# ScalarE takes a convolution's unshifted tap and two levels of copies; heads are squared and gated out of PSUM, and output norms start from partial sums

## The chip, the cores and the metric

One core of one Trainium2 chip. The metric is the device time of the whole program in microseconds (us), the median of several runs. Everything is float32; TensorE's large products are split in software into a "high" and a "low" half (`h_high`, `h_low`, `w_high`, `w_low`), three matmuls for each block.

## The reference, cut to what matters

Four layers run on a sequence of 256 tokens of width 1024: an HGRN-2 mixer, an RG-LRU mixer (each followed by a product-key expert layer), then an "even" mixer (gated delta rule beside dilated attention) and an "odd" mixer (differential attention beside gated linear attention, GLA), each followed by a convolutional feed-forward layer. The pieces that the change touches:

```python
# HGRN-2 (8 heads, both directions) and GLA (4 heads): decayed attention by chunks
attn = sum_k(q[t, k] * k[s, k] * decay[t, s, k]);  o = attn @ v + carried state
o = rms_norm(o, norm_g) * silu(g);  y = o @ w_out
# delta rule: q, k, v pass a causal convolution of width 4 before everything else
y = w[0] * xp[:, :seq];  for j in 1..3: y = y + w[j] * xp[:, j:j + seq]
o_a = rms_norm_2(o_a, norm_w) * silu(z_a);  mix = concatenate([o_a, o_b]) @ w_out
# after an output product: residual and norm
x = x + g1 * y;  h = rms_norm(x, g) * (1 + sc) + sh          # hg_out, lru_out
h = layer_norm(ALPHA * h + mix, g, b)                        # even_out, odd_out
```

## The kernel before

The activations lie transposed: 128 features on the partitions, 256 tokens (`T`) along the free axis, eight chunks (`DC`) for the width. Weights come from memory as tiles of 128x1024 through a ring of four (SP's queue). For a split product ScalarE writes `w_high` of tile k+2 (`split_high`, two halves, each as soon as half of tile k is used), VectorE subtracts to get `w_low` (`split_low`), and TensorE runs 24 matmuls (`passes`, L528 to L530) for the tile into one of four PSUM slots. There is no planner around the change: each engine runs one fixed list of instructions, and semaphores tie the lists together.

**Decayed attention** (`decay_attention`, used for HGRN-2 as `HG` and for GLA). The score matrix of a chunk of 128 tokens is built from a diagonal and seven levels of blocks, for HG once for each of two directions; a last step crosses the two chunks. For each step n TensorE computes scores (L670) into `PB` or `PA` by turns. VectorE multiplies keys and queries by the decay of the next level (`spread`, L1851 to L1860, which waits until the scores that used them are done) and moves the blocks of the level out of PSUM under a mask (`select`, L1873). ScalarE copies only the crossing scores (L1271). Then TensorE computes the output (L682, L686) into `PA`. In order after it: VectorE copies `PA` to SBUF (L2438, for GLA L2394), ScalarE squares the copy (L1191), TensorE sums the squares (L619), ScalarE takes the root (L1251), VectorE the reciprocal (L1803), TensorE spreads it over the partitions (L627), and VectorE multiplies each pair of heads by it (L1810), by gain and gate (L1817; L1815 for the differential heads), and splits it (`split_pair`, L1766) after ScalarE's L1165. TensorE waits for all pairs of L1810 before the output product starts. The delta rule ends in the same `head_norm`, with its squares taken from PSUM by ScalarE and its copy (L2324) beside the sums.

**The output products** (`hg_out`, `lru_out`, `even_out`, `odd_out`). VectorE adds each finished chunk to `X` (`add_product`, L1708 and L1709). For the first two ScalarE squares pairs of chunks (L1191) and TensorE adds up the eight chunks in eight matmuls against a matrix of 1/D (L602). For the last two the mean comes first (L611, eight matmuls over `X`), VectorE subtracts it (L1792), and then come squares and L602. A root (L1195), a reciprocal (L1758), a scaling and an affine step lead to the next product.

**The delta rule's convolution** (tiles 18 to 35 of the 42 of `even_in`). VectorE writes the unshifted tap of each tile from PSUM (L1686) and adds three shifted ones (L1684). In the tiles before, 0 to 17, ScalarE evacuates the product (L1414) and then splits the tile after next; some of both carry steps of the dilated attention. At tile 36 ScalarE waits for the last convolution and goes on with tables for Silu and the squares that lead to the delta rule.

## Time and profile before

| | us |
|---|---|
| median of 3 runs (lowest, highest) | 3133.36 (3130.40, 3135.28) |
| the profiled execution | 3136.99 |
| its span, first to last instruction | 3135.3 |
| TensorE busy | 2956.2 (94%) |
| VectorE busy | 2258.7 (72%) |
| ScalarE busy | 1614.1 (51%) |
| mean granted TensorE clock | 0.963 of full |

Busy times are sums over a span in which many stages follow each other; the granted clock is TensorE's, as a share of 2.4 GHz, and 0.50 is 1.2 GHz. The stages that the change touches lie at 200 to 345 us (HG and `hg_out`), 1300 to 1333 (`lru_out`), 2286 to 2390 (convolution), 2467 to 2515 (end of the delta rule, `even_out`) and 2826 to 2915 (GLA, `odd_out`).

### The profile page before, as it was taken

To read this page: it belongs to the slowest core of one execution; us is meant where nothing else is said; L and a number is where in the kernel's file an instruction comes from. 1 tells how busy PE (TensorE), PEld (TensorE's weight loads), DVE (VectorE), ACT (ScalarE), POOL (GpSimd) and SP (SyncE) were. 2 spreads that over 40 slices of the span, in tenths; PEclk is the share of its full clock that TensorE was granted. 3 is DMA by queue.
4 is the path that set the end of the run, shared out by engine and by line. 5 is a ranking of instruction groups with operands and counts; after the bars stand their busy time and mean duration, and the time that the engine had idled before them with its cause. 6 is when DMAs were issued, how large, how long until landed. Compare 5 with 4: busy or idle time off the path is not lost.

```text
span 3135.3 us, 57437 instructions
## 1 busy us (share of the span) xinstructions
PE 2956.2 (94%) x19454; PEld 2691.2 (86%) x19454; DVE 2258.7 (72%) x4758; ACT 1614.1 (51%) x3321; POOL 79.0 (3%) x120
## 2 busy tenths in 40 slices
PE   5997999999999999989999999999999889897898
PEld 4886899999887778889999988887898889796896
DVE  6337579888779984459888877777685578665686
ACT  1111557778644443455777854444543257462574
POOL 3000000000001100000000000000200000000000
PEclk8998999999999999999999999999899999997999
DMA  9520455444468863445444455554331145441453
GB/s 365 198 92 14 138 178 169 154 158 148 154 238 312 308 208 114 142 149 186 162 150 161 142 174 188 188 190 164 136 125 54 55 165 171 137 140 56 138 176 121
DMA packets 137685, 502.97 MB, mean 160 GB/s; under 512 B 15312, under 2 KB 15440, under 8 KB 137264
## 3 DMA queue, kind: packets, MB, share of 16 engines
q1 hardware_dynamic: 122544, 445.57, 41.8%
q0 software_dynamic: 14976, 55.19, 4.9%
q8 instruction: 106, 1.74, 0.2%
q14 instruction: 59, 0.48, 0.0%
HBM read 498.60 MB, written 2.10 MB: 160 GB/s over the span
## 4 chain that ended last, share of the span: by engine, by line
PE 81%; DVE 6%; ACT 3%; issue 1%; DVEq 0%; ACTq 0%
PE PB L528 13%; PE PB L530 13%; PE PB L529 13%; PE PA L570 9%; PE PA L572 9%; PE PA L571 9%; PE PA L722 4%; PE PB L518 3%; DVE w_low L2097 2%; PE PA L929 1%; PE PA L602 1%; PE PA L1092 1%; DVE BIG L2123 1%; ACT h_high L1234 1%; PE PB L929 1%
## 5 line engine op out<-in xcount | busy, mean ns | idle before, releaser
L1131 ACT ACTIVATE w_high<-ring 128x512 fp32r<-128x512 f32 x1532 | 953.4, 630 | 869.3 <-PE PA L572 466.9
L2097 DVE TENSOR_TENSOR w_low<-ring,w_high 128x512 fp32r<-128x512 f32 x1532 | 1047.8, 695 | 433.4 <-ACT w_high L1131 420.3
L528 PE MATMUL PB<-h_high,w_low 128*128 128x256 f32 x3728 | 1081.5, 290 | 48.6 <-DVE h_low L1766 35.8
L530 PE MATMUL PB<-h_high,w_high 128*128 128x256 f32 x3728 | 1059.2, 284 | 0.0
L529 PE MATMUL PB<-h_low,w_high 128*128 128x256 f32 x3728 | 1059.0, 284 | 0.0
L528 PEld LDWEIGHTS PB<-h_high,w_low 128*128 128x128 f32 x3728 | 725.5, 195 | 66.8 <-issue 54.3
L529 PEld LDWEIGHTS PB<-h_low,w_high 128*128 128x128 f32 x3728 | 714.8, 192 | 0.0
L530 PEld LDWEIGHTS PB<-h_high,w_high 128*128 128x128 f32 x3728 | 713.6, 191 | 0.0
L570 PE MATMUL PA<-w_low,a_high 128*128 128x512 f32 x1200 | 475.5, 396 | 11.0 <-DVE a_low L2106 10.5
L572 PE MATMUL PA<-w_high,a_high 128*128 128x512 f32 x1200 | 473.8, 395 | 0.0
L571 PE MATMUL PA<-w_high,a_low 128*128 128x512 f32 x1200 | 473.8, 395 | 0.0
L570 PEld LDWEIGHTS PA<-w_low,a_high 128*128 128x128 f32 x1200 | 226.3, 189 | 71.1 <-DVE a_low L2106 10.7
L572 PEld LDWEIGHTS PA<-w_high,a_high 128*128 128x128 f32 x1200 | 226.9, 189 | 51.9
L571 PEld LDWEIGHTS PA<-w_high,a_low 128*128 128x128 f32 x1200 | 226.8, 189 | 51.8
L518 PE MATMUL PB<-H,ring 128*128 128x256 f32 x896 | 200.7, 388 | 2.6 <-ACT H L1235 2.6
L518 PEld LDWEIGHTS PB<-H,ring 128*128 128x128 f32 x896 | 174.5, 195 | 27.5 <-issue 2.7
L722 PE MATMUL PA<-onehot_b,onehot_a 128*128 128x128 f32 x1024 | 137.5, 277 | 2.9 <-issue 2.6
L2106 DVE TENSOR_TENSOR a_low<-BIG,a_high 128x256 fp32r<-128x256 f32 x300 | 127.6, 425 | 10.3
L722 PEld LDWEIGHTS PA<-onehot_b,onehot_a 128*128 128x128 f32 x1024 | 124.7, 191 | 6.7 <-issue 3.3
L1726 DVE SCALAR_TENSOR_TENSOR BIG<-BIG,coef 128x1024 f32<-128x1024 f32 (+1 forms) x84 | 107.7, 1282 | 16.5 <-DMA BIG<-ada 14.9
L1319 ACT ACTIVATE onehot_a<-inv,slots 128x128 f32<-128x128 f32 x256 | 111.0, 481 | 0.0
L2123 DVE SCALAR_TENSOR_TENSOR BIG<-PB,par,BIG 128x255 f32 (+3 forms) x176 | 84.4, 480 | 14.8 <-DVE BIG L2123 14.5
(324 smaller groups left out, 2652.0 us busy)
## 6 DMA issues: line engine op xcount, KB each, us to landing
ring<-tiles SPq DMA_DIRECT2D x842, 512.0 KB, 3.3
BIG<-ada POOLq DMA_DIRECT2D x96, 512.0 KB, 6.2
BIG<-skew POOLq DMA_DIRECT2D x4, 512.0 KB, 4.5
X<-x SPq DMA_DIRECT2D x1, 1024.0 KB, 6.1
skew<-BIG POOLq DMA_DIRECT2D x1, 1024.0 KB, 9.3
out<-X SPq DMA_DIRECT2D x4, 256.0 KB, 2.0
con<-consts SPq DMA_DIRECT2D x1, 853.0 KB, 8.9
BIG<-masks POOLq DMA_DIRECT2D x1, 768.0 KB, 7.8
```

The source lines that it names most:

```text
L518: ins = mm(product_slot(q0 + i), wt[:, k * P:(k + 1) * P], src[:, k * T:(k + 1) * T], start=k == 0, stop=k == DC - 1)
L528: mm(dst, lhs_l, high, start=start, stop=False, skip_group_check=True)
L529: mm(dst, lhs_h, low, start=False, stop=False, skip_group_check=True)
L530: return mm(dst, lhs_h, high, start=False, stop=stop, skip_group_check=True)
L570: mm(dst, high[:, own], w_l, start=first, stop=False, skip_group_check=True)
L571: mm(dst, low[:, own], w_h, start=False, stop=False, skip_group_check=True)
L572: ins = mm(dst, high[:, own], w_h, start=False, stop=last, skip_group_check=True)
L722: ins = mm(PA[:, (g % 4 * 4 + i) * P:(g % 4 * 4 + i + 1) * P], onehot_a[:, i * P:(i + 1) * P], onehot_b[:, i * P:(i + 1) * P], start=True, ...
L1131: fn(tile_half(w_high, s, b), ring[:, at:at + HALF], ACT.Identity).then_inc(sem("high_ready"), 1)
L2097: tt(tile_half(w_low, s, b), ring[:, at:at + HALF], tile_half(w_high, s, b).bitcast(F32), ALU.subtract).then_inc(sem("low_ready"), 1)
L2106: tt(pair(a_low, j), a, pair(a_high, j).bitcast(F32), ALU.subtract)\
L2123: stt(dst, product_slot(q0 + j)[:, 0:T - sh], wt[tap][:, bass.ds(it * 4 + j, 1)], dst, ALU.mult, ALU.add).then_inc((taken, sem("conv_step" ...
```

## The change

- Convolution: ScalarE writes the unshifted tap, scaled by its weight, for tiles 18 to 35, before it splits tile k+2; VectorE waits for it (`conv_begun`) and adds the three shifted taps.
- Decayed attention: the blocks of levels 5 and 6 are whole rectangles of 32 and 64 rows; ScalarE copies them from PSUM, after VectorE's last select; VectorE doesn't select them.
- Ends of HG and GLA: the output is released by pairs of heads. ScalarE squares a pair from PSUM, VectorE multiplies it from PSUM by gain and gate into SBUF, and TensorE's sums are laid between the outputs. The four differential heads are summed by TensorE just before GLA's output, and scaled by their gain in one instruction. After the root each pair needs one multiplication. The delta rule's copy becomes that multiplication by gain and gate.
- Norms after the four output products: VectorE adds up chunks during the product. The squares' sum has four matmuls in place of eight (`hg_out`, `lru_out`), the mean two in place of eight (`even_out`, `odd_out`).

```diff
+COPIED = (PAIR_LEVELS - 2, PAIR_LEVELS - 1)
...
-            def mean_squares(dst, of=SQUARES):
-                for k in range(DC):
-                    if k % 2 == 0:
+            def mean_squares(dst, of=SQUARES, first=0):
+                if first:
+                    pe.wait_ge(sem("partial_ready"), w.up(sem("partial_ready")))
+                    w.up(sem("squares_ready"), first // 2 + 1)
+                for k in range(first, DC):
+                    if k % 2 == 0 and (k > first or not first):
                         pe.wait_ge(sem("squares_ready"), w.up(sem("squares_ready")))
-                    ins = mm(dst, c("mean_d"), of[:, k * T:(k + 1) * T], start=k == 0, stop=k == DC - 1)
+                    ins = mm(dst, c("mean_d"), of[:, k * T:(k + 1) * T], start=k == first, stop=k == DC - 1)
                 ins.then_inc(sem("mean_square_ready"), 1)
             def rms(name=None):
-                mean_squares(norm_bank(name, 0), squares_for(name))
+                mean_squares(norm_bank(name, 0), squares_for(name), DC - 4 if name in product_at else 0)
             def layer_norm(name):
-                for k in range(DC):
+                if name in product_at:
+                    pe.wait_ge(sem("partial_ready"), w.up(sem("partial_ready")))
+                    mm(norm_bank(name, 1), c("mean_d"), inv[:, :], start=True, stop=False)
+                for k in range(DC - 1 if name in product_at else 0, DC):
...
+            def spread_heads(n):
                 pe.wait_ge(sem("head_inverse"), w.up(sem("head_inverse")))
                 for h in range(0, n, 2):
                     spread_roots(n, h, h * T)
-                pe.wait_ge(sem("heads_scaled"), w.up(sem("heads_scaled"), n // 2))
-            def decay_attention(cfg):
+            def heads_scaled(n):
+                pe.wait_ge(sem("mix_pairs"), w.up(sem("mix_pairs"), n // 2))
+            def decay_attention(cfg, sq, before=0):
...
+                def sums(first, many):
+                    pe.wait_ge(sem("head_squares"), w.up(sem("head_squares")))
+                    head_sums(rows_of, sq, first, many)
...
-                    if n >= 2:
+                    if 2 <= n < selected + 2:
                         pe.wait_ge(masked, masked0 + n - 1)
+                    elif n >= 2:
+                        pe.wait_ge(sem("decay_copied"), copied0 + n - 1 - selected)
...
-                pe.wait_ge(masked, w.up(masked, len(order) - len(ways)))
-                pe.wait_ge(sem("decay_cross_ready"), w.up(sem("decay_cross_ready"), len(ways)))
+                if before:
+                    sums(0, before)
+                pe.wait_ge(masked, w.up(masked, selected))
+                pe.wait_ge(sem("decay_copied"), w.up(sem("decay_copied"), len(order) - selected))
...
-                ins.then_inc(sem("decay_out"), 1)
+                    if h % 2:
+                        ins.then_inc(sem("decay_out"), 1)
+                    if h % 2 and h > 4:
+                        sums(before + h - 5, 2)
+                for h in range(max(0, nh - 4), nh, 2):
+                    sums(before + h, 2)
...
+            def decayed_squares(sq, n):
+                for i in range(n // 2):
+                    act.wait_ge(sem("decay_out"), w.up(sem("decay_out")))
+                    squares(two(PA, i), two(sq, i), "head_squares")
...
+                act.wait_ge(masked, w.up(masked, 1 + COPIED[0] * many))
+                for lev in COPIED:
+                    half = 1 << lev
+                    for d in range(many):
+                        of_lev = 1 + lev * many + d
+                        act.wait_ge(scores, of + of_lev + 1)
+                        for at in range(0, P, 2 * half):
+                            rows = slice(at + d * half, at + (d + 1) * half)
+                            cols = slice(at + (1 - d) * half, at + (2 - d) * half)
+                            ins = fn(blocks(cfg["at"], nm)[rows, :, :, cols],
+                                     blocks((PB, PA)[of_lev % 2][:, :], 2048 // per // P)[rows, :, :, cols],
+                                     ACT.Identity)
+                        ins.then_inc(sem("decay_copied"), 1)
...
+                    else:
+                        if j == SWA_TILES:
+                            act.wait_ge(taken, q0 + j)
+                        act.wait_ge(tile_done, r0 + j + 1)
+                        fn(big(j * T, T), product_slot(q0 + j), ACT.Identity,
+                           scale=p("gdn_conv_w", 3 * 18 + j - SWA_TILES, 1)).then_inc(sem("conv_begun"), 1)
...
+                    if begun is None:
+                        dve.wait_ge(tile_done, it * u + (r0 + i + 1))
+                        if bias is None:
+                            ins = ts(whole, ps, wc, None, ALU.mult)
+                        else:
+                            ins = ts(whole, ps, wc, bias[:, bass.ds(it * u + i, 1)], ALU.mult, ALU.add)
+                        ins.then_inc(sem("conv_step"), 1)
+                    else:
+                        dve.wait_ge(begun, it * u + i + 1)
...
-                        if q:
-                            dve.wait_ge(sem("conv_step"), it * (u * per) + (s0 + i * per + q))
-                            ins = stt(out_, src, wc, out_, ALU.mult, ALU.add)
-                        elif bias is None:
-                            ins = ts(out_, src, wc, None, ALU.mult)
-                        else:
-                            ins = ts(out_, src, wc, bias[:, bass.ds(it * u + i, 1)], ALU.mult, ALU.add)
-                        ins.then_inc(sem("conv_step") if q < per else taken, 1)
+                        if q or begun is None:
+                            dve.wait_ge(sem("conv_step"), ready + (q if begun else q + 1))
+                        ins = stt(out_, src, wc, out_, ALU.mult, ALU.add)
+                        ins.then_inc(sem("conv_step") if q < len(shifted) - 1 else taken, 1)
...
+                def add_up(k, out, a, b):
+                    if k > 1:
+                        dve.wait_ge(step, w.value(step))
+                    if k < last:
+                        w.up(step)
+                    tt(out, a, b, ALU.add).then_inc(sem("partial_ready") if k == last else step, 1)
+                last = DC - 2 if gate is None else 2
...
+                    if gate is None and 2 <= m < DC - 1:
+                        for k in range(m - 1, m + m // (DC - 2)):
+                            dve.wait_ge(taken, q0 + k + 1)
+                            add_up(k, inv[:, :], X[:, 0:T] if k == 1 else inv[:, :], X[:, k * T:(k + 1) * T])
+                    elif gate is not None and m in (4, 6):
+                        k = m // 2 - 1
+                        dve.wait_ge(sem("squares_ready"), squared + k + 1)
+                        add_up(k, two(of, k), two(of, k - 1), two(of, k))
...
-            def head_norm(o, n, gain, gate, gated=0):
+            def gated_heads(o, n, gain, gate):
+                for i in range(n // 2):
+                    dve.wait_ge(sem("head_squares"), w.up(sem("head_squares")))
+                    for h in (2 * i, 2 * i + 1):
+                        s_ = slice(h * T, (h + 1) * T)
+                        ins = stt(o[:, s_], PA[:, s_], gain(h), gate[:, s_], ALU.mult, ALU.mult)
+                    ins.then_inc(sem("dve_step"), 1)
+                    w.up(sem("dve_step"))
+            def scale_heads(o, n):
                 inverse_heads(n)
+                dve.wait_ge(sem("dve_step"), w.value(sem("dve_step")))
                 for i in range(n // 2):
                     dve.wait_ge(sem("head_scales"), w.up(sem("head_scales")))
-                    tt(two(o, i), two(o, i), two(PA, i), ALU.mult).then_inc(sem("heads_scaled"), 1)
-                    dve.wait_ge(sem("heads_scaled"), w.up(sem("heads_scaled")))
-                    for h in (2 * i, 2 * i + 1):
-                        oh = o[:, h * T:(h + 1) * T]
-                        if h < gated:
-                            ins = ts(oh, oh, gain(h), 1.0 - LAM_INIT, ALU.mult, ALU.mult)
-                        else:
-                            ins = stt(oh, oh, gain(h), gate[:, (h - gated) * T:(h - gated + 1) * T],
-                                      ALU.mult, ALU.mult)
-                    ins.then_inc(sem("mix_pairs"), 1)
...
-                        select(n - len(ways), *order[n - len(ways)])
+                        if order[n - len(ways)][0] not in COPIED:
+                            select(n - len(ways), *order[n - len(ways)])
...
-                    v.tensor_copy(chunks(e["mix"][:, 0:6 * T])[:, :, t * P:(t + 1) * P],
-                                  chunks(gdn_bank(2 + t), P)).then_inc(sem("dve_step"), 1)
-                dve.wait_ge(sem("dve_step"), w.up(sem("dve_step"), TT))
-                head_norm(e["mix"][:, 0:6 * T], 6, lambda h: p("gdn_norm_w"), e["z"])
+                    own = slice(t * P, (t + 1) * P)
+                    stt(chunks(e["mix"][:, 0:6 * T])[:, :, own], chunks(gdn_bank(2 + t), P), p("gdn_norm_w"),
+                        chunks(e["z"])[:, :, own], ALU.mult, ALU.mult).then_inc(sem("dve_step"), 1)
+                w.up(sem("dve_step"), TT)
+                scale_heads(e["mix"][:, 0:6 * T], 6)
...
-                v.tensor_copy(e["mix"][:, 4 * T:8 * T], PA[:, 0:4 * T]).then_inc(sem("heads_ready"), 1)
-                dve.wait_ge(sem("heads_ready"), w.up(sem("heads_ready")))
+                dve.wait_ge(sem("head_squares"), w.up(sem("head_squares")))
+                ts(e["mix"][:, 0:4 * T], e["mix"][:, 0:4 * T], p("diff_norm_w"), 1.0 - LAM_INIT, ALU.mult, ALU.mult)\
+                    .then_inc(sem("dve_step"), 1)
+                w.up(sem("dve_step"))
                 dve.wait_ge(sem("gate_silu"), w.up(sem("gate_silu")))
-                head_norm(e["mix"], 8, lambda h: p("diff_norm_w" if h < 4 else "gla_norm_w"), e["r"], 4)
+                gated_heads(e["mix"][:, 4 * T:8 * T], GLA_HEADS, lambda h: p("gla_norm_w"), e["r"])
+                scale_heads(e["mix"], 8)
```

## Rows read from the trace of the kernel before

**Rows 1.** The page's busy time, share of the span and instructions of each engine:
```profile
PE 2956.2 (94%) x19454; PEld 2691.2 (86%) x19454; DVE 2258.7 (72%) x4758; ACT 1614.1 (51%) x3321; POOL 79.0 (3%) x120
```

**Rows 2.** Timeline, HG's levels: start, us, engine, line, tiles, count [idle before <-releaser]:
```profile
258.28 2.43 DVE L1873 COPY_PREDICATED BIG<-way_masks,PB 128x2048 f32<-128x2048 uint32 x1
260.61 2.34 DVE L1851 TENSOR_TENSOR BIG<-BIG 128x1024 f32<-128x1024 f32 x2
...
260.85 3.81 PE L670 MATMUL PB<-BIG 128*128 128x128 f32 x32 [0.92 <-DVE BIG L1873]
...
281.66 0.77 PE L682 MATMUL PA<-BIG 128*128 128x128 f32 x2 [1.21 <-ACT BIG L1271]
```

**Rows 3.** Timeline, the end of HG:
```profile
291.13 2.29 DVE L2438 COPY BIG<-PA 128x2048 f32<-128x2048 f32 x1 [10.88 <-PE PA L686]
293.46 1.91 ACT L1191 ACTIVATE BIG<-BIG 128x2048 f32<-128x2048 f32 x1 [11.95 <-DVE BIG L2438]
...
295.42 5.31 PE L619 MATMUL PB<-BIG,con 128*8 128x256 f32 x16 [4.32 <-ACT BIG L1191]
...
301.36 1.74 DVE L1803 RECIPROCAL inv<-inv 8x256 f32<-8x256 f32 x1 [7.93 <-ACT inv L1251]
...
303.15 7.19 PE L627 MATMUL PA<-inv,con 8*128 8x256 f32 x16 [2.43 <-DVE inv L1803]
...
312.36 0.55 PE L528 MATMUL PB<-h_high,w_low 128*128 128x256 f32 x1 [2.02 <-DVE BIG L1810]
```

**Rows 4.** Stretches: from:to, length, busy us of each engine, granted clock, DMA share, GB/s:
```profile
281.00:291.00 10.00, 9.34 (x64) 9.28 (x64) 0.00 (x0) 0.51 (x1) 0.00 (x0) 0.75 0.24 78
303.00:312.00 9.00, 7.19 (x16) 5.14 (x16) 6.60 (x14) 1.89 (x3) 0.00 (x0) 0.50 0.00 0
...
2254.00:2286.00 32.00, 32.00 (x244) 29.51 (x244) 24.07 (x38) 16.59 (x36) 0.00 (x0) 1.00 0.40 132
2286.00:2362.00 76.00, 76.00 (x597) 71.23 (x597) 68.62 (x133) 34.36 (x60) 0.00 (x0) 1.00 0.38 131
...
2870.00:2874.00 4.00, 3.40 (x14) 2.94 (x15) 2.71 (x7) 0.63 (x1) 0.00 (x0) 0.91 0.00 0
```

**Rows 5.** Timeline, the end of GLA:
```profile
2855.65 0.77 PE L682 MATMUL PA<-BIG 128*128 128x128 f32 x2 [0.79 <-ACT BIG L1271]
...
2860.50 1.22 DVE L2394 COPY BIG<-PA 128x1024 f32<-128x1024 f32 x1 [3.19 <-PE PA L686]
...
2870.59 4.60 PE L627 MATMUL PA<-inv,con 8*128 8x256 f32 x16 [2.43 <-DVE inv L1803]
...
2878.10 0.55 PE L528 MATMUL PB<-h_high,w_low 128*128 128x256 f32 x1 [2.90 <-DVE BIG L1810]
```

**Rows 6.** Timeline, the end of the delta rule:
```profile
2474.73 2.98 PE L627 MATMUL PA<-inv,con 6*128 6x256 f32 x12 [2.40 <-DVE inv L1803]
2480.66 0.55 PE L528 MATMUL PB<-h_high,w_low 128*128 128x256 f32 x1 [2.94 <-DVE BIG L1810]
```

**Rows 7.** Timeline, norms behind the output products:
```profile
332.08 1.88 ACT L1191 ACTIVATE BIG<-X 128x512 f32<-128x512 f32 x3
...
337.00 3.62 PE L602 MATMUL PA<-BIG,con 128*128 128x256 f32 x16
...
2502.30 0.42 DVE L1708 SCALAR_TENSOR_TENSOR X<-X,PB 128x256 f32<-128x256 f32 x1 [1.14 <-PE PB L530]
2505.12 0.42 DVE L1708 SCALAR_TENSOR_TENSOR X<-X,PB 128x256 f32<-128x256 f32 x1 [2.41 <-PE PB L530]
2505.58 1.29 DVE L2097 TENSOR_TENSOR w_low<-ring,w_high 128x512 fp32r<-128x512 f32 x2
2508.58 2.48 DVE L1792 TENSOR_TENSOR X<-X,PA 128x512 f32<-128x512 f32 x4 [1.71 <-PE PA L611]
```

**Rows 8.** Timeline, ScalarE at tile 36, behind the convolution:
```profile
2361.59 1.28 ACT L1414 ACT_TABLE_LOAD   x1 [3.25 <-DVE BIG L1684]
2362.88 0.38 ACT L1414 ACTIVATE BIG<-PB 128x256 f32<-128x256 f32 x1
```

More of the change, by code:

```diff
@@ L1543, in odd_mixer @@
                 decay_attention(GLA)
[L1544 to L1545 removed]
+                decayed_squares(e["sq"][:, 4 * T:8 * T], GLA_HEADS)
                 head_roots(8, 1.0 / P)
@@ L1664, in loop, with convolution @@
                     body(i, 0)
-            def convolution(name, n, dst, weight, taps, shifts, bias, u=8, first=0):
+            def convolution(name, n, dst, weight, taps, shifts, bias, u=8, first=0, begun=None):
                 q0, r0 = product_at[name][0] + first, STREAM_AT[name][0] + first
-                s0, per = w.value(sem("conv_step")), len(shifts) - 1
+                s0, per = w.value(sem("conv_step")), len(taps) - (2 if begun else 1)
                 if q0 > 0:
                     dve.wait_ge(taken, q0)
-                order = [taps.index(0)] + [i for i in range(len(taps)) if taps[i] != 0]
+                shifted = [i for i in range(len(taps)) if taps[i] != 0]
                 def body(i, it):
-                    dve.wait_ge(tile_done, it * u + (r0 + i + 1))
-                    ps = product_slot(q0 + i)
-                    for q, tap in enumerate(order):
+                    ps, ready = product_slot(q0 + i), it * (u * per) + (s0 + i * per)
+                    whole = dst[:, bass.ds(it * (u * T) + i * T, T)]
+                    wc = weight(taps.index(0))[:, bass.ds(it * u + i, 1)]
+                    if begun is None:
[7 more added lines that the diff above has]
+                        dve.wait_ge(begun, it * u + i + 1)
+                    for q, tap in enumerate(shifted):
                         sh = taps[tap]
```

60 lines of the change are left out of this document (31 added, 29 removed).

## The prediction

> **What bounds the kernel now.** I read the page's busy times first, then the timeline around each place that the diff touches, then the granted clock of those stretches. TensorE is busy 94% of the span [rows 1], so time can be won only where it waits, or where it works off something that needn't stand on the path. Two kinds of stage are to be told apart. In the convolution TensorE is busy 76.00 of 76 us, though VectorE is too (68.6) [rows 4]: work taken off VectorE there is hidden. In the ends of the attentions and the norms the engines take turns: each row of [rows 3] begins where the one before it ends, with TensorE idle before the sums, before the spreading and before the output product. There every microsecond counts once. Each stage ends in a product that TensorE starts at once, so the gains of the stages add up.
>
> An fp32 matmul stands in the records as two, so "x16" is eight matmuls. Eight of 256 columns take 3.62 us at the full clock [rows 7], 0.45 each, and twice that at half. An operation of VectorE on 512 columns goes by in 0.65 (1.29 for two), one on 256 in 0.42, and VectorE's additions follow each other 2.82 apart, the time of one tile of a split product [rows 7].
>
> **HG, levels 5 and 6.** Before, a step costs one select and one spread, 2.43 + 2.34 = 4.7 us [rows 2], while TensorE needs 3.8 for its scores, and 3.6 (16 matmuls of 128 columns) where groups follow each other. Four selects go (two levels, two directions). The last score group before that is the one at 260.85, which still waits for a select. Behind it TensorE runs groups 13 and 14 back to back: 260.85 + 3 x 3.6 = 271.6. The VectorE spreads (2.3, begun 0.2 behind each scores' end) and ScalarE's copies (1024 columns, half of the 1.91 for squares of 2048 [rows 3], some 1.1 in the two pieces of level 5) both fit beside one group. The crossing groups then end at 273.5 and 275.4, ScalarE's last copy at 276.6, and the output starts at 276.75 against 281.66 [rows 2]: 4.9 us. The copies were not seen in this shape; if a rectangle cost what a whole copy of 2048 columns does (1.91 for squares [rows 3]) they would still end before the group that needs them. Bounds 3.5 and 5.5.
>
> **HG, output to spreading.** Before: output 281.66 to 290.9, copy 2.29, squares 1.91, sums 5.31, root, reciprocal 1.74, spreading at 303.15 [rows 3]. The copy goes. The squares of pairs 0 to 2 lie beside the output, and that of pair 3 (some 0.65) beside TensorE's sums of the pairs before. The gating on VectorE (0.9 for a pair) lies beside sums and root. TensorE has output and sums in a row: 9.3 as before, with the same slow part, and 3.6 for the sums at full clock, as no idle stretch of 4.5 us (290.9 to 295.42) stands ahead of them. That gives 276.75 + 12.9 = 289.65, 0.6 for the root (from the end of L619, 300.73, to 301.36) and 1.8 for the reciprocal: 292.1. Against 303.15 it is 11.05, of which 4.9 are the levels' and 6.15 new.
>
> **HG, spreading to product.** Before 303.15 to 312.36, 9.2 us, with the clock at 0.50 throughout [rows 4] and VectorE doing a multiplication, two gatings and a split for each pair. After, a pair of spreads takes 1.0 at full clock (2.98 for three [rows 6]), and VectorE then has four multiplications and two splits before TensorE's wait ends: 1.2 + 6 x 0.65 + 0.3 = 5.4. That is 3.8 less. The full clock is my choice: after sums and an idle 2.4 us the spreading ran fast in GLA (0.91 [rows 4]) and in the delta rule [rows 6]. At half clock it is some 8.1, 1.1 less.
>
> **GLA.** The levels gain nothing: there VectorE's spread waits for the scores with nothing to select in the way, and the last copy stays ScalarE's. The sums of the four differential heads now stand between the last scores (2854.9) and the output, ahead of it: 3.5 us at the half clock of that stretch, against 0.8 of waiting. They are paid back behind it. After: 3.5, output 3.3 (4.7 before, until L2394, mostly at half clock; the stretch without a gap now begins earlier), sums of two pairs 1.8: 2863.5, and with root and reciprocal 2.4 the spreading at 2865.9 against 2870.59 [rows 5], 4.7 less. If the clock doesn't rise in between, it is 2.2 less. ScalarE's table load (1.28 [rows 8]) lies beside the last sums. From spreading to product 7.5 [rows 5] becomes 5.4 as above: 2.1. The one scaling of the differential heads (1024 columns, near 1 us) fits VectorE's pause before the output's first pair. GLA 6.8 in all.
>
> **Delta rule's end.** The copy beside the sums becomes a gating of the same size, so nothing changes up to the spreading. From 2474.73 to 2480.66, 5.9 us [rows 6], it becomes 1.2 + 4 x 0.65 + 0.3 = 4.1: 1.8.
>
> **Norms.** *hg_out*: the eight matmuls (3.62 [rows 7]) all ran behind the product. After, two work on the partial sum while VectorE adds the last chunk and ScalarE squares it (1.4), two follow (0.9): 2.4, so 1.2 less. But the adding at chunk 4 waits for squares that ScalarE does only after it has split tile 7 (332.08, three in 1.88 [rows 7]: the second ends at 333.3). VectorE then adds (334.0) and only then lowers tile 7 (334.65), which TensorE wants at 334.2, 2.82 before 337.0. That costs 0.5; left 0.7. *lru_out* has no tiles to split during the product, but the root needs a table load behind the last square: 1.4 + 1.28 = 2.7 for 3.6, 1.0 less. *even_out, odd_out*: the mean ended 3.4 behind the product, its last matmul would now end after 1.6. What is late next is VectorE's `split_low` (2505.58 + 1.3 = 2506.9 against 2508.58 for L1792 [rows 7]): 1.7 each. VectorE's seven additions per product (0.45 each) lie in its pauses. Together 5.1, bounds 3 and 6.5.
>
> **Convolution.** 18 operations on 256 columns go from VectorE (0.42 for such a one [rows 7]), 18 of 0.38 [rows 8] come to ScalarE, and TensorE, the bound, sees neither. What is left is the end: at tile 36 ScalarE waited for VectorE's last tap until 2361.59 [rows 8], and its chain sets the pace from there. VectorE lags there by some 0.3 a tile over the last tiles without attention work, as its 3.1 us a tile (two lowerings and four taps) stand against 2.82. ScalarE will wait for product 36 itself. I take 0.6; the bounds are 0 and the whole wait of 3.25. If the cover went (the last rival) it would cost.
>
> A rule speaks against the roots moved forward. The Trainium skill (ScalarE: Activation LUTs, "What ACT_TABLE_LOAD costs") puts a switch of tables at about 1.28 us and a drain of 1.38 more. By it three roots (HG, GLA, lru_out) would come up to 1.4 later, and the gain would be 4 us smaller, an estimate from that page. The trace has 1.28 and the next activation 0.01 behind it (2361.59, 2362.88 [rows 8]), and the measurement decides.
>
> **Sum.** 4.9 + 6.15 + 3.8 (HG) + 6.8 (GLA) + 1.8 (delta rule) + 5.1 (norms) + 0.6 = 29.2 us. The profiled execution took 3136.99, 3.6 over the median of the runs shown; off its time it is 3107.8, off the median 3133.36 it is 3104.
>
> **Rivals.** *The clock stays up.* The idle time of TensorE, in and behind which the clock fell to half, shrinks. If it holds, HG's output wins 2.1 (a stretch with mean 0.75 [rows 4]), and the starts of three output products win. HG's eight tiles took 24.6 (312.36 to 337.00 [rows 3, 7]) where 8 x 2.82 is 22.6, so 2 each: 8 more, 3096. For it: in the delta rule the idle time ahead of the product falls from 2.94 [rows 6] to about 1.1. Against: the spreads use 6 or 8 rows of the array, and the clock fell during 7.19 us of them in HG. The Trainium skill (TensorE: Matmul & The Clock Gate, Part 1) calls the throttled state the default and says that activity releases it; its rule stands behind this case.
>
> *The clock stays down.* Spreading at half clock in all three places (2.7 + 2.7 + 1.8), HG's sums no faster than 5.31 (1.7), GLA without its rise (2.5): 11.4 less gain, 3115.6. For it: the whole of GLA's levels and HG's spreading ran at half. Against: [rows 4, 6] as above.
>
> *Slower: ScalarE's tap starves TensorE.* At tile k ScalarE split the first half of tile k+2 while product k was still running; now it waits for its end, copies (0.38), splits (0.63), and VectorE lowers (0.69): 1.8 with handing over, and if three taps of VectorE (1.4) and an exponential of ScalarE (768 columns, near 1) stand in the way too, 4.3, against 2.8 that product k+1 covers. 1.5 late on each of 18 tiles is 27; with the attention's three operations on 768 columns (2.5 on five tiles) in the same line it is 39.5, and the kernel ends at 3144. It decides from 1.65 us a tile (29.2 / 18). Against: in 2254 to 2286 ScalarE has the same order, evacuation first, with the attention's steps, and TensorE was busy 32.00 of 32 [rows 4].
>
> **Chances.** The forecast 0.63 (own range 3099 to 3110), clock up 0.18, clock down 0.13, the starving 0.03 (it ends slower), anything else that eats the gain 0.03, most of it still faster. A measurement can tell 0.2%, 6.3 us, from no change. Faster 0.95, same 0.02, slower 0.03, as the starving is the only case that ends there. The range reaches to the two clock cases, whose ends also cover the bounds of the levels and norms: 3094 to 3117.
>
> **What would show it.** Counted from the score group that follows select 10, HG's output starts at +15.9 instead of +20.8 us; L627 starts 15.3 us behind the output's start (before 21.5), and the product 5.4 behind L627. In GLA four L619 stand ahead of L682, and from the last scores to the end of the sums it takes 8.6 us. TensorE does four matmuls of L602 for hg_out and lru_out, and two for the mean of the others, with L1792 released by VectorE's own L2097. In the convolution TensorE stays busy 76 of 76. If TensorE waits for `w_low` there on more than a few tiles, or if no stretch between output and product gets shorter, I am wrong.

## The result, and the profile after

The kernel after takes 3109.72 us (median of 4 runs, 3105.24 to 3115.05), before 3133.55 (3130.4 to 3135.28): a ratio of 0.9926, 95% interval 0.9908 to 0.9943. That is 23.8 us less; forecast were 29.2, and 3104.0 for the time. The profiled execution took 3115.05 (span 3113.4), 21.9 less than that of before in the span. Its busy row, against [rows 1]:

```profile
PE 2946.5 (95%) x19414; PEld 2682.0 (86%) x19414; DVE 2242.1 (72%) x4739; ACT 1624.3 (52%) x3352; POOL 80.4 (3%) x120
```

TensorE is busy 9.7 us less in the records; the other 12 came out of its waits. The end of HG in the timeline of after (start, us, engine, line, tiles, count, [idle before <-releaser]), for [rows 2, 3]:

```profile
260.20 3.81 PE L687 MATMUL PB<-BIG 128*128 128x128 f32 x32 [0.91 <-DVE BIG L1955]
...
271.00 1.95 PE L687 MATMUL PA<-BIG 128*128 128x128 f32 x16
...
275.94 0.46 PE L701 MATMUL PA<-BIG 128*128 128x128 f32 x2 [1.21 <-ACT BIG L1318]
...
284.62 2.54 PE L626 MATMUL PB<-BIG,con 128*8 128x256 f32 x11
285.13 1.28 ACT L1280 ACT_TABLE_LOAD   x1
...
287.20 0.46 ACT L1280 ACTIVATE inv<-PB,con 8x256 f32<-8x256 f32 x1 [0.79 <-PE PB L626]
287.70 1.74 DVE L1884 RECIPROCAL inv<-inv 8x256 f32<-8x256 f32 x1 [1.68 <-ACT inv L1280]
289.49 4.29 PE L634 MATMUL PA<-inv,con 8*128 8x256 f32 x16 [2.33 <-DVE inv L1884]
...
295.05 0.55 PE L529 MATMUL PB<-h_high,w_low 128*128 128x256 f32 x1 [1.26 <-DVE BIG L1901]
```

From the score group to the output it is 15.74 us (20.81 before), from the output to the spreading 13.55 (21.49), from there to the product 5.56 (9.21). The copy of 2.29 is gone, the sums begin while the output still runs, and the table load lies beside them.

The output alone ran faster than before: 281:291 stood at a clock of 0.75 [rows 4]. That is not the change's doing. The kernel b_fill (below) has the same instructions as the kernel before up to HG's sums, and in its execution, with the same wait of 1.21 ahead, the output ran at full clock:

```profile
280.09 0.46 PE L690 MATMUL PA<-BIG 128*128 128x128 f32 x2 [1.21 <-ACT BIG L1279]
```

```profile
280.00:290.00 10.00, 7.38 (x64) 7.22 (x64) 2.29 (x1) 0.16 (x1) 0.00 (x0) 1.00 0.26 84
```

There it is 20.23 us from the score group to the output and 19.44 from the output to the spreading. Of the gains of HG, 2.6 us (0.57 and 2.05) are the slow clock of the one execution of before that was profiled.

The end of the delta rule, first of before (for [rows 6]), then of after, and the norm behind its product in after:

```profile
2469.58 2.76 PE L619 MATMUL PA<-BIG,con 128*6 128x256 f32 x12 [0.90 <-ACT BIG L1191]
...
2509.98 3.72 PE L602 MATMUL PA<-SQUARES,con 128*128 128x256 f32 x16 [1.44 <-ACT SQUARES L1191]
```

```profile
2450.74 2.75 PE L626 MATMUL PA<-BIG,con 128*6 128x256 f32 x12 [0.90 <-ACT BIG L1220]
...
2455.83 4.82 PE L634 MATMUL PA<-inv,con 6*128 6x256 f32 x12 [2.33 <-DVE inv L1884]
...
2461.81 0.55 PE L529 MATMUL PB<-h_high,w_low 128*128 128x256 f32 x1 [1.17 <-DVE BIG L1901]
...
2486.74 0.59 PE L615 MATMUL PA<-inv,con 128*128 128x256 f32 x2
2487.41 0.70 PE L618 MATMUL PA<-X,con 128*128 128x256 f32 x2
2490.00 5.41 PE L606 MATMUL PA<-SQUARES,con 128*128 128x256 f32 x16 [1.89 <-ACT SQUARES L1220]
```

The mean now takes two matmuls as planned. But the spreading took 4.82 where it had taken 2.98, and the eight sums of squares 5.41 where the same eight took 3.72 before (all 16 records, in both `even_out` and `odd_out`).

GLA, for [rows 5]. Its last score group, the start of the GLA row of the table below, in before:

```profile
2853.63 1.23 PE L670 MATMUL PB<-BIG 64*128 64x128 f32 x8 [0.59 <-DVE BIG L1860]
```

In after:

```profile
2836.08 1.23 PE L687 MATMUL PB<-BIG 64*128 64x128 f32 x8 [0.59 <-DVE BIG L1942]
2837.24 3.58 PE L626 MATMUL PB<-BIG,con 128*8 128x256 f32 x8
...
2840.75 1.22 PE L701 MATMUL PA<-BIG 128*128 128x128 f32 x4
...
2844.33 1.89 PE L626 MATMUL PB<-BIG,con 128*8 128x256 f32 x8
2845.05 1.28 ACT L1280 ACT_TABLE_LOAD   x1
...
2846.35 0.47 ACT L1280 ACTIVATE inv<-PB,con 8x256 f32<-8x256 f32 x1
...
2848.64 6.80 PE L634 MATMUL PA<-inv,con 8*128 8x256 f32 x16 [2.42 <-DVE inv L1884]
...
2856.61 0.55 PE L529 MATMUL PB<-h_high,w_low 128*128 128x256 f32 x1 [1.17 <-DVE BIG L1901]
```

Here the spreading went from 4.60 to 6.80, and from it to the product it is 7.97, before 7.51. The granted clock, for [rows 4] (from:to, length, busy us of PE, PEld, DVE, ACT, POOL, then PEclk, DMA share, GB/s):

```profile
275.00:281.00 6.00, 5.06 (x45) 5.09 (x46) 1.46 (x4) 1.99 (x3) 0.00 (x0) 1.00 0.56 171
281.00:290.00 9.00, 6.67 (x39) 3.95 (x39) 3.78 (x6) 2.94 (x4) 0.00 (x0) 1.00 0.01 2
...
2456.00:2462.00 6.00, 4.83 (x13) 3.36 (x14) 3.27 (x5) 1.86 (x3) 0.00 (x0) 0.54 0.00 0
2490.00:2496.00 6.00, 5.41 (x16) 4.14 (x16) 2.28 (x4) 2.22 (x4) 0.00 (x0) 0.72 0.49 169
2808.00:2837.00 29.00, 18.75 (x144) 16.37 (x144) 16.32 (x31) 7.99 (x12) 0.00 (x0) 0.62 0.00 1
...
2855.00:2861.00 6.00, 4.83 (x22) 4.43 (x21) 2.71 (x5) 1.38 (x3) 0.00 (x0) 0.50 0.01 3
```

HG's output runs at the full 2.4 GHz here; the delta rule's spreading, the sums of squares and the start of GLA's output product stand wholly or partly at 1.2.

By landmarks (us gained between the two profiled executions; each is the start of one TensorE instruction against another):

| stage | forecast | measured |
|---|---|---|
| HG, score group to output | 4.9 | 5.07 |
| HG, output to product | 9.95 | 11.59 |
| `hg_out`, product to next product | 0.7 | 0.57 |
| `lru_out`, sums of squares to next product | 1.0 | 0.99 |
| convolution, up to the start of tile 38 | 0.6 | 1.06 |
| delta rule, head sums to product | 1.8 | 0.01 |
| `even_out`, product to next product | 1.7 | -0.56 |
| GLA, last scores to product | 6.8 | 3.94 |
| `odd_out`, product to next product | 1.7 | -0.21 |
| sum | 29.2 | 22.5 |

The long products between these stages differ by up to 4 us between executions of any of the kernels, either way; the table leaves that out. The four rows that fell short (8.8 us together) are those in which the same matmuls took longer in after than in before, at a lower clock (the spreadings 4.82 for 2.98 and 6.80 for 4.60, the sums of squares 5.41 for 3.72 twice). The two HG rows hold the 2.6 us of clock named above; against an output at full clock they would be 4.5 and 9.5, a little under the forecast.

### The profile page after: what moved, and what is told of

Read it like the earlier page. It is cut to its first block, busy times and chain, and to the rows that moved or that the text cites. A ratio compares the mean times of both kernels' runs of the same rounds, so it can differ in the third digit from the quotient of the medians.

```text
span 3113.4 us, 57380 instructions
## 1 busy us (share of the span) xinstructions
PE 2946.5 (95%) x19414; PEld 2682.0 (86%) x19414; DVE 2242.1 (72%) x4739; ACT 1624.3 (52%) x3352; POOL 80.4 (3%) x120
## 4 chain that ended last, share of the span: by engine, by line
PE 81%; DVE 5%; ACT 4%; issue 1%; DVEq 0%; ACTq 0%
PE PB L529 13%; PE PB L530 13%; PE PB L531 13%; PE PA L571 9%; PE PA L573 8%; PE PA L572 8%; PE PA L746 4%; PE PB L519 3%; DVE w_low L2179 2%; PE PA L953 1%; PE PA L1121 1%; PE PA L606 1%; PE PA L634 1%; ACT h_high L1263 1%; DVE BIG L2205 1%
```

## The experiments

Theory: the delta rule's row and the three below it fall short because TensorE's clock halves there, not because of a new wait. Rival: an engine or a longer wait holds the product back. Fillers below are matmuls whose result nobody reads.

**a_again**: the kernel after once more.

> The changed kernel once more, for a second trace and on the same chip as the next three. If the gain that is missing against the forecast (some 7 us in the traced execution) is TensorE's clock, the same five stages run at half clock again: the spreading at the end of the delta rule (4.8 us where full clock gives 3.0) and of GLA (6.8), and the squares' sums behind even_out and odd_out (5.4 each where full clock gives 3.7). If it was an accident of that execution, they differ in the second trace. Time: 3106 to 3113 either way.

3110.54 us, ratio 0.9931 (0.9919 to 0.9943). The delta rule's end in this execution:

```profile
2445.91 2.75 PE L626 MATMUL PA<-BIG,con 128*6 128x256 f32 x12 [0.90 <-ACT BIG L1220]
2450.99 3.06 PE L634 MATMUL PA<-inv,con 6*128 6x256 f32 x12 [2.33 <-DVE inv L1884]
2455.35 0.55 PE L529 MATMUL PB<-h_high,w_low 128*128 128x256 f32 x1 [1.30 <-DVE BIG L1901]
```

The same program with the same waits spread in 3.06 instead of 4.82, and head sums to product took 9.44 instead of 11.07: the 1.6 us of this step come and go with the clock. Here the expectation, that all of these stages would be slow again, missed. The GLA spreading (6.99) and both sums of squares (5.41) were slow again, and so they were in a_select below (6.97, 5.41), so these are not chance. The time was as expected.

**a_mean8**: the mean by eight matmuls over `X` again, without VectorE's partial sum (`False and` leaves it out).

```diff
-                if name in product_at:
-                    pe.wait_ge(sem("partial_ready"), w.up(sem("partial_ready")))
-                    mm(norm_bank(name, 1), c("mean_d"), inv[:, :], start=True, stop=False)
-                for k in range(DC - 1 if name in product_at else 0, DC):
+                for k in range(DC):
...
-                    if gate is None and 2 <= m < DC - 1:
+                    if False and gate is None and 2 <= m < DC - 1:
```

> The changed kernel, but the means behind even_out and odd_out are again eight matmuls over X. Clock theory: the six additional matmuls keep TensorE at full clock, the squares' sum behind them takes 3.7 in place of 5.4, and the mean ends 1.75 later; from the end of the product to the next product each stage stays as it is in the changed kernel within 0.3 us, and so does the whole time. Rival (the partial sums gain their 1.75 a stage, and the loss lies elsewhere): 3.5 us slower than the changed kernel.

3114.75 us, ratio 0.9933 (0.9915 to 0.9952). The sums of squares are at full clock again behind a busy TensorE:

```profile
2483.74 3.61 PE L615 MATMUL PA<-X,con 128*128 128x256 f32 x16
2488.79 3.72 PE L606 MATMUL PA<-SQUARES,con 128*128 128x256 f32 x16 [1.44 <-ACT SQUARES L1217]
```

Product to next product is 39.91 and 40.32 us, in the kernel after 39.67 and 40.18: taking 2.2 us of matmuls out of the mean gained 0.2. In after the sums start 0.45 later behind the mean (1.89 of waiting for 1.44) and take 1.69 more. The time can't decide here: by the medians a_mean8 is 4.2 us slower than a_again, nearer to the rival's 3.5 than to the account's nothing, but its four runs go from 3105.16 to 3116.39, and the two ratios are alike. The landmarks decide for the account.

**a_fill**: matmuls that nobody reads (128x256; five, ten records, take 2.42 us at full clock) in TensorE's waits: five ahead of each spreading, two behind it, four between mean and squares.

```diff
+            def fill(n, of=PB):
+                for _ in range(n):
+                    mm(of[:, 768:1024], c("mean_d"), c("ident", 0, 2 * P), start=True, stop=True)
             def spread_heads(n):
+                fill(5, PA if n == GDN_HEADS else PB)
                 pe.wait_ge(sem("head_inverse"), w.up(sem("head_inverse")))
                 for h in range(0, n, 2):
                     spread_roots(n, h, h * T)
+                fill(2)
...
                 ins.then_inc(sem("mean_ready"), 1)
+                if name in product_at:
+                    fill(4)
                 mean_squares(norm_bank(name, 0))
```

> The changed kernel plus matmuls whose result nobody reads, put where TensorE would idle: five ahead of each spreading (in the 2.4 us of root and reciprocal), two behind it, four between mean and squares behind even_out and odd_out. Clock theory: the spreadings take 3.0 (delta rule) and 4.3 (GLA, HG), the squares' sums 3.7 each, the output products start at full clock: 1.8 + 2.5 + 3.4 and up to 2 for each product start, 3098 to 3103. Rival (these stages are slow for another reason, or the idle time isn't what the clock follows): nothing gets shorter, and the fills in TensorE's order cost up to 1 us a place: 3110 to 3114.

3105.56 us, ratio 0.9912 (0.9900 to 0.9925), against 0.9931 for the kernel after on the same chip:

```profile
2451.98 2.85 PE L636 MATMUL PA<-inv,con 6*128 6x256 f32 x12
2454.76 1.35 PE L642 MATMUL PB<-con 128*128 128x256 f32 x4
2456.33 0.55 PE L529 MATMUL PB<-h_high,w_low 128*128 128x256 f32 x1 [0.22 <-issue]
...
2481.41 1.89 PE L642 MATMUL PB<-con 128*128 128x256 f32 x8
2483.46 3.72 PE L606 MATMUL PA<-SQUARES,con 128*128 128x256 f32 x16 [0.16 <-ACT SQUARES L1228]
```

Nothing that VectorE or ScalarE does was shortened, and the stages are faster: head sums to product 9.44, `even_out` to the next product 36.92 (39.67), GLA's last scores to product 17.58 (20.53), `odd_out` 36.99 (40.18). That is 8.9 us by landmarks, and 1.6 more where the delta rule's spreading had been slow; 5.0 in the medians, 8.1 between the spans of a_again and a_fill. The time came out above the account's 3098 to 3103 and below the rival's 3110. Not all of it is the fillers': 1.5 of GLA's 2.95 lie ahead of its spreading, before any filler of that stage (last scores to spreading 11.05 for 12.56, as the first sums ran in 2.78 for 3.58), and the spreading itself took 5.09, not the 4.3 expected. Behind the fillers it is spreading to product 6.54 for 7.97, and sums of squares 3.72 for 5.41 in both norms. There the theory is shown: no engine's wait was taken away, TensorE was only kept from idling in them.

**a_fill2**: twelve more behind the sums of squares.

```diff
                 mean_squares(norm_bank(name, 0), squares_for(name), DC - 4 if name in product_at else 0)
+                if name in product_at:
+                    fill(12)
...
                 mean_squares(norm_bank(name, 0))
+                if name != "down1":
+                    fill(12)
```

> As the one before, and twelve such matmuls more behind the squares' sums of hg_out, lru_out, even_out, odd_out and the first feed-forward layer, where TensorE waits 6 us for the next layer's first pair. Clock theory: the next product no longer starts at half clock; the pairs come 1.97 us apart and hide it until the fourth, so 0.9 us a place, 4.5 in all over the kernel before it. Rival: the fills delay the first pair's matmuls and win nothing.

3107.47 us, ratio 0.9915 (0.9902 to 0.9927): no gain over a_fill, as the rival had it. Behind `even_out` the first two pairs of the next product ran at 0.95 us instead of 1.62, but they wait for VectorE's splits anyway, and from the third pair on the clock was at half again.

**b_tap**: the kernel before with ScalarE's tap alone (`convolution` and the loop that feeds it as in the change; the diff stands there).

> The kernel before with one part of the change alone: in the delta rule's convolution the tap without a shift is put in place by ScalarE, and VectorE adds the shifted three; norms and ends of the attentions stay as before. My account (the tap was off TensorE's path but for the end, where ScalarE waited on VectorE's last tap): TensorE busy 76 of 76 us in the stretch, no wait on the lowered tiles, tile 38 starts 0.6 to 1.1 us earlier against the first tile of the convolution, and the end of the kernel comes at most 1 us earlier, ratio 0.9997, inside what can be measured. Rival (ScalarE's tap starves TensorE): waits on the lowered tiles behind each product of the convolution, 1.5 us each or 27 us in all, ratio 1.009. Second rival (VectorE was the bound and the whole wait goes): 3.2 us earlier at the end, ratio 0.999.

3134.12 us, ratio 1.000 (0.9991 to 1.001). The windows row of the convolution and ScalarE at tile 36, against [rows 4, 8]:

```profile
2286.00:2362.00 76.00, 76.00 (x597) 71.23 (x596) 60.84 (x116) 40.63 (x81) 0.00 (x0) 1.00 0.40 131
```

```profile
2359.47 1.28 ACT L1414 ACT_TABLE_LOAD   x1 [2.02 <-DVE BIG L1701]
2360.76 0.39 ACT L1414 ACTIVATE BIG<-PB 128x256 f32<-128x256 f32 x1
```

VectorE gives up 7.8 us, ScalarE takes 6.3, TensorE has no gap: nothing starves. The wait for the last tap went from 3.25 to 2.02. Counted from the end of tile 17's product, tile 38's ends 1.0 us earlier (83.90 for 84.92) and the head sums behind it begin 1.15 earlier. Then these sums ran at half clock (5.28 for 4.44), and the delta rule's own head sums come only 0.2 earlier by the same count (186.58 for 186.78). The spreading behind them took 5.16 for 2.98, in instructions that are the same as before's: its fast spreading was a chance as well.

**a_select**: the kernel after, with VectorE selecting all of HG's levels again.

```diff
-COPIED = (PAIR_LEVELS - 2, PAIR_LEVELS - 1)
+COPIED = ()
+CHOSEN_LEVELS = PAIR_LEVELS - len(COPIED)
...
-                selected = 1 + COPIED[0] * len(ways)
+                selected = 1 + CHOSEN_LEVELS * len(ways)
...
-                act.wait_ge(masked, w.up(masked, 1 + COPIED[0] * many))
+                act.wait_ge(masked, w.up(masked, 1 + CHOSEN_LEVELS * many))
```

> The kernel after, but HG's two last rectangle levels are selected and spread by VectorE again (none copied by ScalarE); all else stays. My account: HG's output starts 4.9 to 5.1 us later against its first level groups than in the kernel after, nothing changes in GLA and the delta rule, and the time comes out 5 us over the kernel after: ratio to the kernel before 0.9945. Rival (the levels are given back by the clock, since a later output runs behind shorter waits): under 2.5 us of the 5 are seen at HG's product, ratio 0.9935. Second rival (VectorE's selects hid ScalarE's copies elsewhere too): over 7 us, ratio 0.9955.

3113.91 us, ratio 0.9935 (0.9919 to 0.9952), 3.4 to 4.2 us over the kernel after's two medians, the second of which was taken on another chip; the ratio alone couldn't tell it from the kernel after:

```profile
281.07 0.46 PE L702 MATMUL PA<-BIG 128*128 128x128 f32 x2 [1.21 <-ACT BIG L1319]
...
300.21 0.55 PE L530 MATMUL PB<-h_high,w_low 128*128 128x256 f32 x1 [1.23 <-DVE BIG L1902]
```

From the score group (here at 260.84) to HG's output it is 20.23 us, in both executions of after 15.74: the levels are worth 4.5, and the rest of the row's 5.07 is the last score group, which in before ran partly at half clock (2.59 us for 2.02). Output to product is 19.14 as in after (19.11), so the rival, that the clock gives the levels back, is out, and the end's gain doesn't depend on the levels.

**a_fill3**: a_fill with more of them behind GLA's score groups.

```diff
                     ins.then_inc(sem("decay_scores"), 1)
+                    if before:
+                        fill(2 if n else 9, lo=1792)
```

> The kernel a_fill (unread matmuls of 256 columns into TensorE's waits: five ahead of each spreading, two behind it, four between mean and squares) with more of them after each score group of GLA's levels: nine after the first, two after each later one, written to a part of the accumulators that nobody reads there. In the kernel after GLA's cycle of 3.09 us ran at half clock with TensorE at work 2.24 us of it. If the half clock sets that cycle (the scores 2.24 us, then VectorE's spread): it goes to 2.0 to 2.4 us, levels 6 to 9 us shorter, ratio to the kernel before 0.989. Rival (VectorE's select and spread set the cycle, at 2.4 to 3.1): levels at most 1 us shorter, ratio 0.991, as a_fill. Second rival (the extra matmuls stand in the way of the next scores, and the clock stays at half): cycle 3.1 + 1 us, levels 8 us longer, ratio 0.994.

3097.74 us, ratio 0.9891 (0.9873 to 0.9909). A cycle of the levels in after, then in a_fill3:

```profile
2817.79 2.24 PE L687 MATMUL PB<-BIG 64*128 64x128 f32 x16 [0.85 <-DVE BIG L1933]
2820.89 2.24 PE L687 MATMUL PA<-BIG 64*128 64x128 f32 x16 [0.85 <-DVE BIG L1933]
```

```profile
2806.23 1.24 PE L695 MATMUL PA<-BIG 64*128 64x128 f32 x16
2807.39 1.13 PE L642 MATMUL PB<-con 128*128 128x256 f32 x4
2808.45 1.26 PE L695 MATMUL PB<-BIG 64*128 64x128 f32 x16
```

The cycle falls from 3.09 to 2.25 us: the scores' own time (2.24, now 1.25) was on the path, at half clock, in after as before. The levels, from the second score group behind the diagonal (2806.23) to the last (2821.97), take 15.7 us for 21.3, so 5.5 less, somewhat under the 6 to 9 expected. The spreading behind them is at full clock as well, and last scores to product takes 16.27 (17.58 in a_fill):

```profile
2832.69 3.71 PE L636 MATMUL PA<-inv,con 8*128 8x256 f32 x16
...
2838.24 0.55 PE L529 MATMUL PB<-h_high,w_low 128*128 128x256 f32 x1 [0.61 <-DVE BIG L1911]
```

**b_fill**: the kernel before, filled as a_fill, but with five matmuls, not two, behind the delta rule's spreading, and three, not four, in the norms.

> The kernel before with unread matmuls of 256 columns in TensorE's waits: five ahead of each spreading, two behind (five in the delta rule), three between mean and squares; nothing of the change. It asks whether what the filling wins is a gain of its own. Account (the clock falls in the waits, in both kernels): HG's spreading falls from 7.19 to 3.7 us, sums to product in HG 3 to 4 us shorter, GLA 2 us, delta rule 1 to 2, in all 5 to 8, ratio 0.998. Rival (the waits before the change were set by VectorE and ScalarE, so the clock's loss was hidden): spreading shorter, products no earlier than 1 us, ratio 0.9997. Second rival (the matmuls delay what they precede): ratio 1.001 or more.

3129.97 us, ratio 0.999 (0.998 to 0.9999), 5.3 less by the medians.

```profile
299.53 4.37 PE L629 MATMUL PA<-inv,con 8*128 8x256 f32 x16
...
307.60 0.55 PE L528 MATMUL PB<-h_high,w_low 128*128 128x256 f32 x1 [1.69 <-DVE BIG L1818]
```

HG's spreading went from 7.19 to 4.37, but the product waited for VectorE (1.69); from spreading to product it is 8.07 for 9.21, and in the delta rule the fillers stood in the way: 12.42 from head sums to product, for 11.08. GLA's last scores to product win 0.3 (24.20 for 24.47), the two norms behind it and behind the delta rule 0.7. So the 5.3 us fit the account's 5 to 8 by luck: its terms (3 to 4 in HG, 2 in GLA, 1 to 2 in the delta rule) came out as 1.1, 0.3 and -1.3. HG's product did come 3.8 earlier against the score group, but 2.6 of that lie ahead of the first filler, in last scores and output at full clock.

**a_fill4 and b_fill4**: the kernels after and before, with fillers at all these places, and at two around the convolution's end; b_fill4 also ahead of the head sums, where before has its own waits.

```diff
                     if j == n - 4:
                         pe.wait_ge(sem("attention_out_taken"), 4 * TT)
+                        fill(7, PA)
                         gdn_squares(0)
...
                 pe.wait_ge(sem("gdn_copied"), GDN_COPIED["values"])
+                fill(4)
                 pe.wait_ge(sem("head_inverse"), w.up(sem("head_inverse")))
```

> The kernel a_fill3 with two more groups of unread matmuls around the end of the convolution: seven in the wait of 3.3 us ahead of the head sums at tile 38, four in the wait of 1.5 us ahead of the delta rule's first spreading. In a_fill3 these sums took 5.28 us (2.75 at full clock elsewhere) and the spreading 7.72, the 48 matmuls behind it 8.2. If the clock is what they cost: sums 2.8 to 4, spreading 3.9 to 5.5, next stages at full clock, 4 to 7 us earlier at the delta rule's head sums, ratio to the kernel before 0.9875. Rival (VectorE's six multiplications of 0.69 set the pace behind each spread): sums shorter but spreading no less than 7, 1 to 2.5 us in all, ratio 0.9885. Second rival (the matmuls themselves delay the sums): nothing gained, 0.989.

> The kernel before with unread matmuls at every such place: ahead of the head sums, of each spreading and behind it, between mean and squares, after each score group of GLA's levels, and at the two places around the convolution's end. It asks what the change is worth when the clock is taken out of the comparison: a_fill4 minus this one. Account: the fills win in both, 10 us of it in GLA's levels and the convolution's end alike, so this kernel lands at 3110 to 3118 (ratio 0.9935), 18 to 24 us over a_fill4; the change's worth without the clock is what the terms of the prediction give apart from the clock. Rival (change and fills win the same time in the ends of the attentions): under 14 us between the two. Second rival (at half clock the change was hindered, it is worth more without): over 28 us.

a_fill4: 3097.47 us, ratio 0.9882 (0.9866 to 0.9898). Against a_fill3 the first head sums took 2.76 instead of 5.28, the spreading 6.83 instead of 7.72, and from these sums to the delta rule's it is 96.84 instead of 99.40. But the kernel after, with no filler there, has sums of 2.75 in both executions, and 98.10 and 96.75 to the delta rule's, so it isn't shown that these fillers won anything; the time doesn't show it either. b_fill4: 3116.56 us, ratio 0.9951 (0.9938 to 0.9965), as expected. Between them lie 19.1 us: that is what the change is worth when fillers stand in the waits of both. By landmarks: HG's score group to output 4.5, output to product 8.4, delta rule 1.7, `even_out` 1.5, GLA 4.1, `odd_out` 2.8, `lru_out` 1.0, `hg_out` 0.3, in all 24.3; in these two executions the stretches between took 6.1 us more in a_fill4, and the spans differ by 18.2. The clock wasn't up everywhere in b_fill4: HG's head sums took 5.31, as in before, though five fillers stand ahead of them, so 1.5 of the 8.4 are clock still (the same sums take 3.79 in after).

a_fill3 and a_fill4 beat both kernels, a_fill4 by 12 us the kernel after and by 36 the one before. a_fill3 is as fast (3097.74), so the gain is that of a_fill (5.0) and of GLA's levels.

## Why the prediction was right, and where it was off

Faster was given 0.95, and the time of 3109.72 lies in the likeliest case's own range, 5.7 over the forecast and just under the range's end (3110). The mechanism held: TensorE's waits in the ends of the attentions and its work in the norms shrank. The clock that was assumed behind them didn't hold in four stages.

*HG's levels* (4.9): 5.07, of which a_select takes back 4.49; the rest is clock. *HG, output to spreading* (6.15): 7.94. The step said "with the same slow part", 12.9 us for output and sums; it was 11.2, as the output ran at full clock. But an output at full clock is found in b_fill and b_fill4 as well, where it is still before's; against them the term is 5.9. So it was sized right, and the 1.8 over it are luck. *Spreading to product in HG* (3.8): 3.65. "The full clock is my choice" was right enough there: the spreading took 4.29 for 16 records (3.71 in a_fill, 7.19 at half), and the faster spreading of a_fill brings the product no nearer (5.56 in both), as VectorE follows with its own 5.

*GLA* (6.8): 3.94. Counted from the last scores the spreading began 4.40 earlier, against 4.7 forecast, so sums ahead of the output were paid back as worked out. The second part, "From spreading to product 7.5 becomes 5.4", is the step that failed: it became 7.97. It was taken over from the stretch at 0.91 in the kernel before [rows 4], which ends at 2874, while that spreading ran on to 2875.20 and the stretch 2874 to 2878 stood at 0.50. In after its clock was 0.5 to 0.6 in both executions (6.80 and 6.99 us). The wait ahead of it is no longer than before (2.42 for 2.43), and TensorE had worked from 2836.08 to 2846.22 without a gap; so why the clock fell there isn't shown, only that it did and what it cost. With fillers it is 5.55 (a_fill3, 2832.69 to 2838.24): the forecast, at the clock that it assumed.

*Delta rule's end* (1.8): 0.01 in one execution, 1.64 in the other, 1.7 between a_fill4 and b_fill4, where both spreadings take 2.85. The work was sized right; whether its gain is seen depends on where the clock falls, in the kernel before (11.08, and 11.89 in b_tap) as in the one after.

*Norms* (5.1): 0.8 by the table. `hg_out` (0.7) with its 0.5 for the late lowering came as worked out: 1.08 won behind the product, about 0.5 lost in it, and TensorE's wait on `w_low` ahead of the last tile is 0.27. `lru_out` 0.99 for 1.0. For the other two the step "its last matmul would now end after 1.6 ... 1.7 each" is right for the mean (it ends 1.2 behind the product) and wrong for the stage: 1.7 us more for the sums of squares, partly at half clock (0.72 over the stretch), 0.45 more of waiting ahead of them, and a product that took 0.3 to 0.7 longer. I had weighed the clock for the spreadings and not for what stands behind a shortened mean.

*Convolution* (0.6): 1.06 in after, 1.0 in b_tap, within the bounds. The starving rival fell: 76.00 of 76 busy.

The table load's drain of the Trainium skill (ScalarE: Activation LUTs, "What ACT_TABLE_LOAD costs") isn't seen: in GLA load and root follow at 2845.05, 1.28, 2846.35, 0.02 apart, and the last sums end at 2846.2, so the root is late by 0.1. The square ahead of the load ends at 2845.04, so there is no drain in front of it either.

The rivals on the clock were put as one case for all stages. In the table it went both ways at once: up in HG's output (+1.8, by before's luck), down in four places (-8.8). *The clock stays down* (3115.6) was the nearer for these.

The same waits ahead of HG's output (2.0 and 1.2 us idle) go with 0.75 in before and b_tap, and with 1.00 in b_fill, b_fill4 and a_select: up to there b_fill is the kernel before, so no difference of the kernels is needed. Open is what decides it in an execution, and why GLA's spreading and the sums of squares were slow every time.

## What to carry to other kernels

Where TensorE's work in a chain of short stages is cut, look at the clock of the stage behind the cut, before counting the gain: a shorter mean bought 1.8 us and lost 1.7 in the next eight matmuls. Price each short stage at both levels of the clock, one by one, and take a second execution of the kernel before too: a stage that was slow by chance there looks like a gain of the change. If TensorE must wait, matmuls that nobody reads, no longer than the wait, can hold the clock; here they gave the changed kernel 12 us, about half of what the change itself did. They don't always: HG's head sums in b_fill4 took 5.31 us behind them, as without.

## What was not expected of the hardware

- TensorE at work 2.24 of each 3.09 us wasn't granted its full clock over GLA's levels (0.62); filled without a gap it was 1.00 from 2806 to 2822 in a_fill3. The Trainium skill (TensorE: Matmul & The Clock Gate, Part 1) has activity release the throttle. The 1.00 of a_fill3 agrees with it, and shows that unread matmuls count as activity.
- The clock of a short stage differs between executions of one program: 4.82 and 3.06 us for the same twelve records with the same wait of 2.33 ahead, and HG's output 9.4 us in before, 7.4 in b_fill, behind the same instructions and waits.
- Spreads with 6 or 8 rows run at full clock behind fillers (2.85 for 12 records, 3.71 for 16), so few rows alone don't pull it down here.
